# Moving tensors between the two halves of the SBUF in a fused two-layer kernel

## The reference, cut to what matters

```python
def first_block(x, c, ...):
    mod = silu(c) @ w_ada + b_ada               # 6 x 1024 modulations
    h = rms_norm(x, g_pre_mix) * (1 + scale1) + shift1
    proj = h @ w_in                             # 1024 x 3584
    mix = concat(y_conv, y_ret) @ w_out         # short convolution, retention
    x = x + gate1 * rms_norm(mix, g_post_mix)
    h = rms_norm(x, g_pre_mlp) * (1 + scale2) + shift2
    f = square(relu(h @ w_fc1)) @ w_fc2         # 1024 -> 4096 -> 1024
    return x + gate2 * rms_norm(f, g_post_mlp)

def second_block(x, ...):
    z = rmsnorm(x, attn_norm_g) @ w_in          # queries, keys, latents, gates
    y_a = sparse attention: top 256 keys of each token by an index score
    y_b = latent attention, 8 heads
    merged = gates0 * (y_a @ w_branch_a) + gates1 * (y_b @ w_branch_b)
    x = x + merged @ w_out
    x = x + square(relu(rmsnorm(x, mlp_norm_g) @ w_ff1)) @ w_ff2
    return rmsnorm(x, final_norm_g)
```

## Time and profile before

| what | value |
|---|---|
| median of 3 runs | 3110.04 us |
| the three runs | 3105.19, 3110.04, 4690.06 us |
| the profiled execution | 3106.66 us |
| its span from first to last instruction | 3104.9 us |
| TensorE busy | 2942.5 us, 95% of the span |
| VectorE, ScalarE, GpSimd busy | 1582.1, 739.5, 1059.7 us |
| mean granted clock of TensorE | 0.963 of full speed |

### The profile page before, as it was taken

One profiled execution on the slowest core, in us unless ns is written; L12 is line 12 of the kernel. 1 busy time (PEld: TensorE's weight loads), 2 busy tenths in 40 slices (PEclk: granted clock), 3 DMA queues, 4 the chain that ended last, 5 costly groups with the idle time before them and its releaser, 6 DMA issues.

```text
span 3104.9 us, 36502 instructions
## 1 busy us (share of the span) xinstructions
PE 2942.5 (95%) x14772; PEld 2384.6 (77%) x14772; DVE 1582.1 (51%) x1842; ACT 739.5 (24%) x1152; POOL 1059.7 (34%) x465
## 2 busy tenths in 40 slices
PE   7999999999999999989979898999989999999997
PEld 7788888778888887767867476777778888888886
DVE  2853235753333337656999534775455233333337
ACT  4101124432001123442101464544122000111101
POOL 1433224444444444442524003100334344444441
PEclk6999999999999999998989998999999999999998
DMA  7441113222111122260312000000421111111111
GB/s 288 141 131 41 41 61 116 75 82 82 48 47 47 47 81 89 75 173 21 85 54 82 26 1 1 2 2 1 156 95 48 48 48 47 47 47 48 47 50 64
DMA packets 250699, 208.55 MB, mean 67 GB/s; under 512 B 20699, under 2 KB 236266, under 8 KB 250058
## 3 DMA queue, kind: packets, MB, share of 16 engines
q1 hardware_dynamic: 247546, 198.37, 20.6%
q10 hardware_dynamic: 3024, 8.39, 0.7%
HBM read 184.84 MB, written 20.97 MB: 66 GB/s over the span
## 4 chain that ended last, share of the span: by engine, by line
PE 78%; DVE 14%; ACT 3%; issue 2%; POOL 1%; SPq 1%; DMA 0%; ACTq 0%; DVEq 0%; POOLq 0%
PE PS L1095 17%; PE PS L1105 16%; PE PS L847 12%; PE PS L1041 8%; DVE MB L2249 6%; PE PS L1057 5%; PE PS L1274 4%; PE PS L831 3%; PE PS L1318 3%; PE PS L1224 2%; PE PS L1248 2%; PE PS L1155 1%; PE PS L924 1%; PE PS L893 1%; DVE FT L2065 1%
## 5 line engine op out<-in xcount | busy, mean ns | idle before, releaser
L723 POOL TENSOR_TENSOR WHI<-RAW,ZERO 128x1024 fp32r<-128x1024 f32 x168 | 321.1, 1911 | 1434.9 <-PE PS L847 460.5
L725 POOL TENSOR_TENSOR WLO<-RAW,WHI 128x1024 fp32r<-128x1024 f32 x168 | 455.5, 2711 | 13.2
L736 POOL TENSOR_TENSOR WLO<-RAW,WHI 128x1024 fp32r<-128x1024 f32 x88 | 212.8, 2419 | 327.9 <-ACT WHI L1440 327.9
L847 PE MATMUL PS<-H,WHI 128*128 128x512 f32 x864 | 271.6, 396 | 12.0 <-DVE L L1775 7.9
L847 PE MATMUL PS<-L,WHI 128*128 128x512 f32 x864 | 268.8, 393 | 0.0
L847 PE MATMUL PS<-H,WLO 128*128 128x512 f32 x864 | 268.3, 392 | 0.0
L1561 ACT ACTIVATE RL<-PS 128x1024 f32<-128x1024 f32 x48 | 49.3, 1027 | 880.1 <-PE PS L1095 880.1
L2161 DVE TENSOR_TENSOR FT<-RL 128x1024 f32<-128x1024 f32 x48 | 91.2, 1900 | 323.4 <-ACT RL L1561 323.4
L1041 PE MATMUL PS<-H,WHI 128*128 128x512 f32 x512 | 204.7, 400 | 8.4 <-POOL WLO L736 7.7
L1041 PE MATMUL PS<-L,WHI 128*128 128x512 f32 x512 | 202.6, 396 | 0.0
L1041 PE MATMUL PS<-H,WLO 128*128 128x512 f32 x512 | 202.2, 395 | 0.0
(11 more groups left out here) (329 smaller groups left out, 5891.6 us busy)
## 6 DMA issues: line engine op xcount, KB each, us to landing
RAW<-w_fc SPq DMA_DIRECT2D x96, 512.0 KB, 3.9
RAW<-w_ff SPq DMA_DIRECT2D x64, 512.0 KB, 3.9
RAW<-w_in SPq DMA_DIRECT2D x62, 512.0 KB, 3.8
ADA<-w_ada SPq DMA_DIRECT2D x32, 512.0 KB, 5.0
RAW<-w_out SPq DMA_DIRECT2D x24, 512.0 KB, 3.7
ADA_FIRST<-w_ada SPq DMA_DIRECT2D x16, 512.0 KB, 9.4
x_scratch<-X SPq DMA_DIRECT2D x2, 4096.0 KB, 16.3
X<-x_scratch SPq DMA_DIRECT2D x2, 4096.0 KB, 12.9
```

The costliest lines, as they stand in the source:

```text
L723: nc.gpsimd.tensor_add(WHI[j][:, 0:n], RAW[j][:, 0:n], ZERO[:, 0:1].to_broadcast([P, n])).then_inc(s_whi, 1)
L725: nc.gpsimd.tensor_sub(WLO[j][:, 0:n], RAW[j][:, 0:n], WHI[j][:, 0:n].bitcast(F32)).then_inc(s_w, 1)
L736: nc.gpsimd.tensor_sub(WLO[w % 2][:, :], RAW[w % 2][:, :], WHI[w % 2][:, :].bitcast(F32)).then_inc(s_w, 1)
L847: last = mm(bank(b + t), wt[:, k, :], a[:, k * S + t * HALF:k * S + (t + 1) * HALF], start=(k == 0 and n == 0), stop=(k == KC - 1 and n == 2))
```

## The change

The order of the tensors in the arena is changed: H, L, then WK (now 13,480 words long, from 16384), then X, Y, RAW, WHI, WLO and the small tensors. By the code the places after are: H 0, L 8192, WK 16384 to 29863, X 29864, Y 38056, RAW 46248, WHI 48296, WLO 50344, small tensors from 52392. FH and FL come to 16384 and 20480. A2H and A2L change regions: A2H now lies on WK (16384) and A2L on Y (38056). F2H and F2L stay on L, now 8192 and 12288. No instruction is added, taken away or put elsewhere; only addresses change.

```diff
--- before.py
+++ after.py
@@ -158,12 +158,15 @@
                 taken[0] += words
             return t
 
-        X0 = taken[0]
-        X = place("X", KC * S)
         H0 = taken[0]
         H = place("H", KC * S, F32R)
         L0 = taken[0]
         L = place("L", KC * S, F32R)
+        K0 = taken[0]
+        WKW = 13480
+        WK = place("WK", WKW)
+        X0 = taken[0]
+        X = place("X", KC * S)
         Y0 = taken[0]
         Y = place("Y", KC * S)
         RAW = [place(f"RAW{j}", 1024) for j in range(2)]
@@ -181,11 +184,7 @@
         SILC = place("SILC", 8)
         ZERO = place("ZERO", 8)
         SSQ = place("SSQ", 8)
-        taken[0] = (taken[0] + 15) // 16 * 16
-        K0 = taken[0]
-        WKW = arena_words - K0 - 16
-        WK = place("WK", WKW)
-        assert WKW >= 13312, WKW
+        assert taken[0] <= arena_words - 16, taken[0]
 
         def region(name, start, words, dt=F32):
             return place(name, words, dt, at=start)
@@ -289,8 +288,8 @@
         GB = [region(f"GB{j}", K0 + 2048 * j, 2 * S) for j in range(4)]
         MT = region("MT", K0 + 8192, 2 * S)
 
-        A2H = region("A2H", Y0, 8 * S, F32R)
-        A2L = region("A2L", K0, 8 * S, F32R)
+        A2H = region("A2H", K0, 8 * S, F32R)
+        A2L = region("A2L", Y0, 8 * S, F32R)
         F2H = region("F2H", L0, 4 * S, F32R)
         F2L = region("F2L", L0 + 4096, 4 * S, F32R)
         F2SUM = region("F2SUM", H0, 8 * S)
```

## The result

The change makes the kernel slower: 3141.68 us (median of 5, 3138.35 to 3143.93) against 3116.02 us (median of 5: 3105.19, 3110.04, 3116.02, 3119.11 and 4690.06). The profiled execution has a span of 3137.5 us against 3104.9. So it is about 1% slower, where 10 us less was forecast.

A forecast was written before the change was run, and what follows sets the result against it. The prediction took TensorE as the bound (busy 95% of the span, 78% of the chain). Savings 5.1 + 3.2 + 1.7 = 10.0 us gave 3110.0 - 10.0 = 3100 us, range 3088 to 3118 (forecast's own 3094 to 3107).

The forecast's parts named there:

- the second of the two readings: fp32r products: a moving operand in the upper half costs because the weights are read from that half at the same time.
- the half theory: fp32r products: the moving operand's SBUF half sets the pace, 226.7 ns a matmul in the lower, 233.3 in the upper.
- Down products of the middle groups: First MLP, line 1105: FH and FL go to the lower half, four groups from 44.79 to 43.52 us, 5.1 us saved.
- Half blocks: Down products at line 1057: 768 times 5.4 ns is 4.1 us, of which 3.2 us was taken as saved.
- Up products of the second MLP: Line 1095, eight groups: A2H goes to the lower half, A2L stays in the upper; 44.16 to 43.95 us, 1.7 saved.
- Products that stream H, L, F2H or F2L: Lines 847, 924, 1041, 1318, other uses of 1095 and 1105: operands stay in the lower half, weights move up; 0.
- Retention, attention and the vector engines: Other tensors that change place: matmuls there stream 128 words or fewer or are whole float32, engine times unchanged; nothing.
- The second: Rival: weights lying higher put 6.6 ns on 6912 matmuls, 45.3 us, plus 5.0 for A2H and A2L; 3160 us, chance 0.08.
- The first rival: Place doesn't matter; the down products' pace comes from something that stays, such as PSUM pairing; time 3110 us, chance 0.12.

The follow-up runs named there:

- e1: Kernel before with only the work region WK (FH, FL, A2L) 32 words further on, still in the upper half; 3097.8 us, ratio 0.9960.
- f4: Kernel before with only A2H and A2L exchanged, A2H on WK and A2L on Y; 3111.72 us in one run, against 3105.54.
- e2: Kernel after with WK 13504 words long in place of 13480, so all large tensors start at multiples of 64 words; 3099.97 us, ratio 0.9972.
- e3: Kernel before with only WHI and WLO 8 words further on, and WK 64 words on; 3142.36 us, ratio 1.0102.
- f3: Kernel before with only WLO (and the small tensors behind it) 32 words on, WK at a multiple of 64; 3135.20 us in one run, against 3105.54.

## Why the prediction was wrong

**What held.** TensorE's pace in the fp32r products is what decides, and it depends on where the operands lie with the instructions unchanged. The surcharge is 6.6 ns of 226.7. It is a matter of both operands (the second of the two readings that the prediction named, that the cost lies between moving operand and weights), though not of their halves. The rows compared on other engines didn't move. The kernel after has FH and F2H written by ScalarE at the same speed:

```profile
L1562 ACT ACTIVATE F2H<-RL 128x1024 fp32r<-128x1024 f32 x32 | 33.9, 1060 | 1.0
...
L1562 ACT ACTIVATE FH<-RL 128x1024 fp32r<-128x1024 f32 x16 | 17.0, 1061 | 0.5
```

and GpSimd still waits for TensorE and not for a DMA:

```profile
POOL WHI L722 <- PE PS L1094: 298.1, 48, 7.7
```

**The step that failed** is the sentence "What goes with the pace is where the moving operand lies: words 8192 to 24575 of the arena". In the kernel before, half and distance go together: all that was fast lay low and at distance 0, all that was slow lay high and at distance 32, and the mixed pair was mixed in both. The reading "in the second, it costs because the weights are read from that half" tied the cost to the pair, but tested no other relation of two addresses than the side. The numbers for it stood in the front part: 39456 - 34816 = 4640, which leaves 32 by 64, while H, L, Y and the weights are all whole multiples. A2H would have been the lever. Most of it lies above the arena's middle (24576 to 32767, the middle at 26550), at distance 0. Six of its eight chunks lie wholly above, so the half theory makes about five of six of its group's matmuls slow (44.6 us by their share), and the distance theory two of six (43.95). Measured was 44.16, nearer to the second, though neither gives it exactly, and the prediction let A2H's place be something in between.

**Term by term.** Down products of the middle groups, -5.1 us: measured 0, since FH and FL went from distance 32 to 24. Half blocks, -3.2 us: the down products gained nothing, and the up products lost 0.61 us per 96. The sizes of both terms were right and their lever wrong: in e1, which brings FH and FL to distance 0, these pieces shrink by 5.1 and 3.1 us, though not all of the second reaches the span. Up products of the second MLP, -1.7 us: measured +3.4 (44.59 against 44.16, eight groups), since A2H went off and A2L came to 0; f4 shows the part of the exchange as 2.8. "Products that stream H, L, F2H or F2L: I take 0": this was the term that mattered, +9.2 us of the span in the second MLP's down products (1.28 a group, and little of it in the last), +5.1 in the middle groups, +5.5 in the last half blocks and the second block's projection, +5.3 in the branch and output products and the second MLP's first group, about +10.2 up to the first MLP's middle groups. Retention, attention and the vector engines were put at nothing; the stretch they fill gave back 5.7 us, as above, with its cause open. The reason given for attention was misread in part: 34 matmuls each of KHH and KLO against QS (lines 1240, 1241) stream 512 words of fp32r. At 6.6 ns they would be worth 0.4 us. WUQ, the row on which that zero rested, was no test: its matmul is a whole float32 one with a median of 592 ns. CQB and WUQ are at distance 32 in the kernel before, 40 in the one after and 0 in e1, and the median is 592 in all three:

```profile
L1195 PE MATMUL PS<-CQB,WUQ x64: 592/592/667, 1719.9 to 1749.6; 128*128 128x512 f32 x64
```

That row is of the kernel after (min, median, max in ns). The pace is read from the starts, since such a duration overlaps the next matmul: these follow each other every 429 ns (median) in all ten runs, at distances 0, 16, 32, 40 and 56. Such a matmul pays nothing at any distance seen.

**The rivals.** The second had the sign, the products concerned and the 6.6 ns right and the cause wrong: e2 has the weights at 48320 and is fast. Its price of 50 us is above the 32.6 measured for two reasons: it took every matmul as being on the path, while the stretches concerned grew by 38.3 us at most, and 5.7 came back in the selection and attention stretch. The first rival's rule, that TensorE never waits on anyone for the SBUF (the Trainium skill, "SBUF — State Buffer", Who interferes with whom), is not contradicted here as to other engines: no run shows such a wait. But what the prediction drew from the page's two independent ports, that addresses are free, does not hold for these matmuls: e3 changes little but the distance between the two operands and costs 1%.

**What stays open.** Why 16 words cost a third and 48 the whole; why the cost spreads from two of six matmuls to their neighbours (44.64 in f3, 44.16 with A2L at 32, 44.36 at 48, 44.37 at 8, where each matmul for itself would give 43.95); and what in the chip has the period of 256 bytes. That the next matmul's weight load and the operand of the running one meet in the memory would be a reason for a cost that hangs on both addresses, but no run shows such a meeting: the weight loads last 188 ns at every distance. That the neighbours pay can be read from the starts in the trace of the kernel before. In the second MLP's up products a matmul of A2L is followed by the next start after 234.0 ns (the first of its pair) or 224.7 (the second), but the four of A2H, all at distance 0, also take 230.5, 227.0, 231.3 and 232.8 ns. They bear more of the surcharge than A2L, the operand that is off.

## What to carry to other kernels

In a stream of fp32r matmuls like these (128x512, each with its own weight load), give moving and stationary operands start addresses that are equal modulo 256 bytes (here: pad every large tensor to a multiple of 64 words); it made 1.4% between e3 (1.0102) and e1 (0.9960), with the same instructions. When two explanations of a pace go together in one trace, look for the one tensor for which they part before pricing either. And when only addresses change, compare the time of long runs of equal matmuls: it repeats to a few hundredths of a us where the total scatters by 10.

## What the runs showed of the hardware that was not expected

In the mean a matmul of 128x512 fp32r words starts every 226.7 ns when its operands are at distance 0 modulo 256 bytes, every 228.9 at 64 bytes (16 words), and every 233.3 to 234.3 at all other multiples of 32 bytes; the weight load shows 188 ns in each case. It can be uneven: at 32 words (FH, FL before) 237.4 and 229.3 ns take turns, at distance 0 all lie within a nanosecond. Which half of the arena the moving operand is in makes no difference (43.52 us for 192 in e1 and e2 in all four products); the weights lay in the upper half in every run. Whole-float32 matmuls of 512 words (592 ns, a start every 429) didn't change with the places, nor did the durations of ScalarE that were compared. TensorE's granted clock in the attention stretch differs between the profiles, 0.93 to 0.96, and moves the total by up to 10 us, nearly as much as the padding of e1 gains.
